# A feed-forward tail: the first pair of the up projection reordered, and the hand-over to the down projection rearranged

## The reference

```python
h = rmsnorm_2(x, norm_ffn_w[l])
u = causal_dwconv(h @ w_up[l], conv_ffn_w[l]) + conv_ffn_b[l]
gate, up = jnp.split(u, 2, axis=-1)
x = x + (jax.nn.silu(gate) * up) @ w_down[l]
return rmsnorm_2(x, norm_final_w)
```

## Time and profile before

| what | value |
|---|---|
| median of 3 runs | 3269.74 us (3268.81 to 3270.42) |
| the profiled execution | 3269.96 us, span 3268.1 us |
| TensorE busy | 3071.9 us, 94% of the span |
| VectorE, ScalarE, GpSimd busy | 1487.5, 815.4, 778.1 us |
| mean granted clock of TensorE | 0.973 |

### The profile page before, as it was taken

How to read it: one execution, slowest core, us unless ns; L and a number is a source line. 1 busy time by engine, 2 the same in 40 slices (tenths; PEclk the granted TensorE clock), 3 DMA queues, 4 the chain that set the end, 5 groups by cost and what they waited for, 6 DMA issues and landing times. The chain is left out here.

```text
span 3268.1 us, 37094 instructions
## 1 busy us (share of the span) xinstructions
PE 3071.9 (94%) x14650; PEld 1742.6 (53%) x14650; DVE 1487.5 (46%) x2481; ACT 815.4 (25%) x1656; POOL 778.1 (24%) x625
## 2 busy tenths in 40 slices
PE   7999999999949999799999998999997999998999
PEld 4457656665424444344456656444444666664444
DVE  2216537674351111524322465314757777774224
ACT  3126524442221111412212126211011222221001
POOL 0004400000000110023022215312606655551323
PEclk8999999999969999899999999999998999999999
DMA  7210000003266987511000130012200112117444
GB/s 291 78 52 29 2 25 2 1 1 136 112 257 244 346 329 270 179 39 39 29 24 28 53 135 2 33 39 82 111 39 39 78 78 78 71 46 284 150 132 135
DMA packets 72316, 334.57 MB, mean 102 GB/s; under 512 B 10960, under 2 KB 12497, under 8 KB 58321
## 3 DMA queue, kind: packets, MB, share of 16 engines
q1 hardware_dynamic: 67536, 315.42, 25.5%
q0 software_dynamic: 4608, 16.78, 2.0%
HBM read 283.92 MB, written 48.23 MB: 102 GB/s over the span
## 5 line engine op out<-in xcount | busy, mean ns | idle before, releaser
L3188 PE MATMUL banks<-down_ring,down_sums 128*128 128x512 f32 x440 | 189.2, 592 | 0.0
L822 PE MATMUL banks<-kT_b,qT_b 96*128 96x512 f32 (+1 forms) x384 | 158.7, 523 | 3.5 <-ACT prob_b L884 2.4
L330 PE MATMUL banks<-w_in,hT 128*128 128x512 f32 (+1 forms) x384 | 157.5, 567 | 1.2 <-PEq L157 1.2
L2905 PE MATMUL banks<-hT,ffn_raw 128*128 128x512 f32 x352 | 156.3, 597 | 1.3 <-PEq L2426 1.3
L728 POOL TENSOR_TENSOR prob<-prob,softmax_columns 128x640 f32<-128x640 f32 (+1 forms) x64 | 75.4, 1199 | 314.6 <-DVE softmax_columns L686 314.6
L3021 DVE SCALAR_TENSOR_TENSOR ffn_acc<-ffn_u,s_ffn_taps,ffn_acc 128x1023 f32<-128x1023 f32 x88 | 129.2, 1479 | 30.4 <-ACT ffn_acc L2962 28.8
L1281 POOL DMA_INDIRECT expert_x<-xn_rows,idxT x16 | 15.7, 983 | 529.6 <-POOLq L1018 522.7
L3188 PEld LDWEIGHTS banks<-down_ring,down_sums 128*128 128x128 f32 x440 | 83.6, 190 | 105.2 <-issue 103.8
L1662 PE MATMUL banks<-hT,side_ring 128*128 128x512 f32 x256 | 127.5, 618 | 1.3 <-PEq L2214 1.3
L1317 PE MATMUL banks<-expert_wg,expert_xT 128*128 128x512 f32 x256 | 114.8, 602 | 2.4 <-ACT expert_xT L1354 1.7
L330 PEld LDWEIGHTS banks<-w_in,hT 128*128 128x128 f32 x384 | 71.8, 190 | 81.8 <-issue 78.5
(11 more groups left out here) (576 smaller groups left out, 6109.8 us busy)
## 6 DMA issues: line engine op xcount, KB each, us to landing
down_ring<-in_w_down SPq DMA_DIRECT2D x132, 256.0 KB, 2.9
expert_wg<-in_w_gate SPq DMA_DIRECT2D x16, 2048.0 KB, 15.2
expert_wu<-in_w_up SPq DMA_DIRECT2D x16, 2048.0 KB, 20.7
expert_wd<-in_w_down SPq DMA_DIRECT2D x16, 2048.0 KB, 8.5
ffn_raw<-in_w_ffn SPq DMA_DIRECT2D x22, 1024.0 KB, 6.1
wmod_slab<-in_w_mod SPq DMA_DIRECT2D x6, 2048.0 KB, 8.0
act_rows<-ffn_acc SPq DMA_DIRECT2D x22, 512.0 KB, 2.6
act_rows<-act_rows SPq DMA_DIRECT2D x22, 512.0 KB, 7.7
```

Of the source, the lines that this page charges most:

```text
L330: last = nc.tensor.matmul(c.ps[:, base + a:base + b], h[:, q, :], k.w_in[i][:, q, 0:b - a], start=q == 0, stop=q == KD - 1)
L822: last = nc.tensor.matmul(scores(u)[:, a:b], heads[u // 2].q[u % 2], heads[u // 2].keys[u % 2][:, a:b], start=True, stop=True, skip_group_ ...
L2905: last = nc.tensor.matmul(c.bank(fi), wt[:, q, :], x[:, q, :], start=q == 0 and m != 2, stop=q == 3, skip_group_check=True)
L3188: return nc.tensor.matmul(c.bank(4 * (p % 2) + t), stationary_of(s)[:, P * t:P * t + P], w[s % RING][:, 0, :], start=j == 0, stop=j == N - 1)
```

## The change

In pair 0 alone TensorE's order becomes 1, 2, 6, 5, 7, 3, 4, and GpSimd's sums come in the order of use: block sums 0, 1 and 2, then four half-width sums for product 6, the in-place one for 7, and four half-width sums each for 7, 3 and 4 (24 instead of 16 instructions, hence the new counts). VectorE makes three of product 6's row sums ahead of T4, and `split(0, 6)` waits for five row sums before its first part and for seven before its last. ScalarE's copies for 6 follow those of product 2.

At the end of `ffn_up` SyncE issues weights for down steps 4 to 7 ahead of rows 10 to 19, GpSimd sums those of steps 4 and 5 as well (`SUMMED` = 6), and the store and read-back of the last two rows leave the stage. In `ffn_down` SyncE first stores these rows from `acc`, issues weights 8 to 11, waits for the store, loads rows 20 and 21, the x tiles and the norm row, and goes on with weights 12.

```diff
     nc = c.nc
-    NP, H, Q, ENDING = NF2 // 2, BANK, BANK // 2, 4
+    NP, H, Q, ENDING, SUMMED, RING = NF2 // 2, BANK, BANK // 2, 4, 6, 8
     w_in = k.ffn_in
     made, rows_summed, w_summed, first_out, corner_out, chained, combined, tapped, conv, silu, done, stored = (
         c.sem(f"ffn_{s}") for s in ("product", "rows_summed", "w_summed", "first_out", "corner_out", "chained", "combined", "tapped", "convolved",
                                     "silu", "done", "stored"))
-    down_summed = c.sem("ffn_down_summed")
+    down_summed = k.down_summed = c.sem("ffn_down_summed")
     B11, B12, B21, B22 = (hT[:, 4 * a:4 * a + 4, H * b:H * b + H] for a in range(2) for b in range(2))
     T1, T2, T4 = (T[:, i, :, :] for i in range(3))
     flat = lambda x: x.rearrange("p q n -> p (q n)")
 
     MADE, COMBINED, SPLIT = 23, 29, (6, 7, 3, 4)
+    ORDER, FIRST_ORDER = (1, 6, 2, 7, 5, 3, 4), (1, 2, 6, 5, 7, 3, 4)
     MADE_AT = {1: 1, 6: 2, 2: 7, 7: 8, 5: 13, 3: 14, 4: 19}
+    FIRST_MADE_AT = {1: 1, 2: 2, 6: 3, 5: 8, 7: 9, 3: 14, 4: 19}
+    FIRST_W, W_AT, FIRST_W_AT = 24, {5: 2, 6: 12, 3: 12, 7: 16, 4: 16}, {5: 2, 6: 10, 7: 16, 3: 20, 4: 24}
     ADDED_AT = {6: 0, 7: 6, 5: 13, 3: 17, 4: 23}
     READ_AT = {6: 4, 7: 10, 3: 21, 4: 27}
     ROWS_AT = {5: 1, 6: 7, 7: 12, 3: 16, 4: 20}
     BANKS = {6: 2, 3: 2, 7: 5, 4: 5}
 
     def ready(p, m, event=0):
-        return MADE * p + MADE_AT[m] + event
+        return MADE * p + (MADE_AT if p else FIRST_MADE_AT)[m] + event
+
+    def w_ready(p, m):
+        return FIRST_W + 16 * (p - 1) + W_AT[m] if p else FIRST_W_AT[m]
 
     def added(p, m, n):
         return COMBINED * p + ADDED_AT[m] + n
             for t in range(2, ENDING):
                 down_weights(t)
             sp.wait_ge(made, MADE * NP)
+            for t in range(ENDING, RING):
+                down_weights(t)
             load(10, 2 * NP - 2)
-            store(NP - 1)
-            sp.wait_ge(stored, 32 * NP)
-            load(2 * NP - 2, 2 * NP)
 
         @block.gpsimd
         def _(pool):
+            def plain_sum(p, i, wait=None):
+                for fi in range(2):
+                    if wait is not None:
+                        pool.wait_ge(w_summed, wait + fi + 1)
+                    out, x, y, op = {0: (sum_of(p, 0, fi), block_of(p, 1, 0, fi), block_of(p, 1, 1, fi), ALU.add),
+                                     1: (sum_of(p, 1, fi), sum_of(p, 0, fi), block_of(p, 0, 0, fi), ALU.subtract),
+                                     2: (sum_of(p, 2, fi), block_of(p, 0, 1, fi), sum_of(p, 1, fi), ALU.subtract),
+                                     7: (block_of(p, 1, 0, fi), block_of(p, 0, 0, fi), block_of(p, 1, 0, fi), ALU.subtract)}[i]
+                    nc.gpsimd.tensor_tensor(out, x, y, op).then_inc(w_summed, 1)
+
+            def sums_of_split(p, ms, at):
+                g = ms[0] in (7, 4)
+                half = slice(0, 2) if len(ms) == 2 else slice(ms[0] in (3, 4), 1 + (ms[0] in (3, 4)))
+                if g:
+                    wide = [raw[p % 2][fi][:, KD:2 * KD, :].rearrange("p (m r) n -> p m (r n)", m=2)[:, half, :] for fi in range(2)]
+                else:
+                    wide = [L1[p % 2][:, 1:3, fi, :, :].rearrange("p m r n -> p m (r n)")[:, half, :] for fi in range(2)]
+                A11, A12, A21, A22 = (wide[fi][:, :, Q * kq:Q * kq + Q] for fi in range(2) for kq in range(2))
+                S1, S2, S4 = (L2[p % 2][g][:, i, half, :, :].rearrange("p m r n -> p m (r n)") for i in range(3))
+                pool.wait_ge(w_summed, at)
+                nc.gpsimd.tensor_tensor(S1, A21, A22, ALU.add).then_inc(w_summed, 1)
+                pool.wait_ge(w_summed, at + 1)
+                nc.gpsimd.tensor_tensor(S2, S1, A11, ALU.subtract).then_inc(w_summed, 1)
+                nc.gpsimd.tensor_tensor(A21, A11, A21, ALU.subtract).then_inc(w_summed, 1)
+                pool.wait_ge(w_summed, at + 2)
+                nc.gpsimd.tensor_tensor(S4, A12, S2, ALU.subtract).then_inc(w_summed, 1)
+
             for p in range(NP):
-                n = 16 * p
                 for fi in range(2):
                     pool.wait_ge(w_in[2 * (p % 2) + fi], 16 * (p // 2 + 1))
                 if p >= 2:
                     pool.wait_ge(made, MADE * (p - 1))
...
-            for t in range(ENDING):
+                n = FIRST_W + 16 * (p - 1) if p else 0
...
+            for t in range(SUMMED):
                 pool.wait_ge(k.down_in[t], 32)
                 nc.gpsimd.tensor_tensor(down[t][:, 0, :], down[t][:, 0, :], down[t][:, 1, :], ALU.subtract).then_inc(down_summed, 1)
...
@@ -2896,7 +2915,7 @@
                     pe.wait_ge(first_out, 2 * p + 2)
                 if m == 5:
                     pe.wait_ge(corner_out, 2 * p + 2)
-                    pe.wait_ge(w_summed, 16 * p + 2)
+                    pe.wait_ge(w_summed, w_ready(p, 5))
...
             def split(p, m):
-                if m in (6, 7):
-                    if p:
-                        pe.wait_ge(combined, added(p - 1, {6: 3, 7: 4}[m], 6))
-                    pe.wait_ge(w_summed, 16 * p + {6: 12, 7: 16}[m])
-                else:
+                if m in (3, 4):
                     pe.wait_ge(combined, added(p, *{3: (6, 6), 4: (7, 7)}[m]))
+                elif p:
+                    pe.wait_ge(combined, added(p - 1, {6: 3, 7: 4}[m], 6))
+                pe.wait_ge(w_summed, w_ready(p, m))
                 if p == 0:
-                    pe.wait_ge(rows_summed, ROWS_AT[m])
+                    pe.wait_ge(rows_summed, ROWS_AT[m] - 2 if m == 6 else ROWS_AT[m])
                 for n in (1, 2, 5, 6, 3, 4, 7):
+                    if p == 0 and m == 6 and n == 7:
+                        pe.wait_ge(rows_summed, ROWS_AT[6])
                     if n in (6, 7):
                         pe.wait_ge(chained, 8 * p + 2 * SPLIT.index(m) + (1 if n == 6 else 2))
                     wt, x = split_factors(p, m, n)
@@ -2925,13 +2945,8 @@
                         last.then_inc(made, 1)
 
             for p in range(NP):
-                plain(p, 1)
-                split(p, 6)
-                plain(p, 2)
-                split(p, 7)
-                plain(p, 5)
-                split(p, 3)
-                split(p, 4)
+                for m in ORDER if p else FIRST_ORDER:
+                    (split if m in SPLIT else plain)(p, m)
...
-                copies(p, 6, 0)
-                copies(p, 6, 1)
+                if p:
+                    copies(p, 6, 0)
+                    copies(p, 6, 1)
                 act.wait_ge(made, ready(p, 2))
                 if p:
                     act.wait_ge(conv, 8 * p)
                 for fi in range(2):
                     nc.scalar.activation(u[:, 0, fi, 0:H], c.bank(fi), ACT.Identity).then_inc(corner_out, 1)
+                if p == 0:
+                    copies(p, 6, 0)
+                    copies(p, 6, 1)
...
+            X11, X12, X21, X22 = halves(T2)
             nc.vector.tensor_tensor(T1, B12, B11, ALU.subtract).then_inc(rows_summed, 1)
             dve.wait_ge(rows_summed, 1)
             nc.vector.tensor_tensor(T2, B22, T1, ALU.subtract).then_inc(rows_summed, 1)
             dve.wait_ge(rows_summed, 2)
+            nc.vector.tensor_tensor(split_rows(6, 0), X12, X11, ALU.subtract).then_inc(rows_summed, 1)
+            dve.wait_ge(rows_summed, 3)
+            nc.vector.tensor_tensor(split_rows(6, 1), X22, split_rows(6, 0), ALU.subtract).then_inc(rows_summed, 1)
+            dve.wait_ge(rows_summed, 4)
+            nc.vector.tensor_tensor(split_rows(6, 2), X21, split_rows(6, 1), ALU.subtract).then_inc(rows_summed, 1)
             nc.vector.tensor_tensor(T4, B21, T2, ALU.subtract).then_inc(rows_summed, 1)
-            split_sums_of(6)
+            dve.wait_ge(rows_summed, 6)
+            nc.vector.tensor_tensor(X12, X22, X12, ALU.subtract).then_inc(rows_summed, 1)
             nc.vector.tensor_tensor(B12, B22, B12, ALU.subtract).then_inc(rows_summed, 1)
             dve.wait_ge(rows_summed, 8)
             split_sums_of(7)
...
+def ffn_down(c, k, d, act_rows, last_rows, w, sums, x, stat, junk, out):
...
-    RING, N, H, READY, ENDING = 8, NF2 // 2, BANK, 4, 4
+    RING, N, H, READY, SUMMED, ENDING = 8, NF2 // 2, BANK, 4, 6, 4
...
-        n_a, n_b = n_a + len(left) - 1, n_b + (len(right) - 1 if s >= READY else 0)
+        n_a, n_b = n_a + len(left) - 1, n_b + (len(right) - 1 if s >= SUMMED else 0)
...
-            for s in range(STEPS):
-                if s >= RING:
-                    wait_used(sp, s - RING)
-                for i, (kh, dh) in enumerate(PRODUCTS[s // N][2] if s >= READY else ()):
+            for f in range(2 * N - 2, 2 * N):
+                sp.dma_start(k.act_dram[f], last_rows[f % 2]).then_inc(rows_out, 16)
+            for s in range(RING, STEPS):
+                wait_used(sp, s - RING)
+                for i, (kh, dh) in enumerate(PRODUCTS[s // N][2]):
```

(21 more changed lines are left out.)

33 lines of the change are left out of this document (13 added, 20 removed).

## The result

The changed kernel takes 3252.18 us (median of 6 executions, 3249.37 to 3259.69), the kernel before 3269.56 in the same session. The ratio is 0.995, 95% interval 0.9937 to 0.9963: 16.3 us less, 12.1 to 20.6. The forecast was 21.5 us less. The direction was right and the gain is some 5 us smaller: from the median of 3269.74 the ratio gives 3253.4, just above the range's upper end of 3253.

What follows compares the result with a forecast made beforehand. TensorE, busy 94% of the span, bounds the kernel, so only its idle stretches pay: 12.1 us at the first pair plus 9.4 at the hand-over make 21.5, from 3269.74 to 3248.2 us, range 3241 to 3253.

Steps and rivals of the forecast that it cites:

- Pair 0's sums: First pair: GpSimd's and VectorE's sums take 21.4 us, so product 6 is let go at 2487.7 (bounds 2485 and 2489.9).
- the model of turns: First pair: GpSimd and VectorE alternate; GpSimd's turn costs 1.27 or 0.73 us, VectorE's 2.06 or 0.43.
- The hand-over: Up to down stage: TensorE idle 1.1 us at full clock instead of 12.38; gain 9.4 us including the step 12 stall.
- a wait of SyncE for the stores that costs nothing: Down stage: stores seen landed at about 3004.5, while weights 8 to 11 keep the queue full until 3009.
- Rival 5: Down stage: SyncE's wait for stores holds up x tiles and weights 12 onwards; landed at 3034 gives 3277.7; chance 0.02.
- Is another wait next?: First pair behind product 6: products 5, 7 and 3 and pair 1's product 6 were all expected without a wait.
- pairs 1 to 10 carry the shift through unchanged: Up projection: full pairs of 44.82 us just move earlier, so the two stretches' gains add.
- 4.6 us of cover: Pair 0: VectorE's adds of 6 end at 2504.2, ahead of product 3 at 2508.8.
- GpSimd, with 12 sums ..., is done by 2521: Pair 1: 12 sums of at most 1.5 us from 2503 finish before product 6 is due at 2527.7; no wait.
- the slow start of product 6: Pair 0: first 8 records after the idle stretch take 3.78 us instead of 1.89; kept as before.
- the stall at step 12: Down stage: TensorE waits 3.5 us for weights 12, then loses 1.6 us to the slow clock.

Runs made afterwards that it cites:

- experiment 4: Changed kernel with product 5 ahead of product 6 in pair 0: 3251.01 us, ratio 0.9944 to the kernel before.
- experiment 7: Changed kernel with ScalarE's first copy for product 4 of pair 0 ahead of its tap: 3255.55 us, ratio 0.9958 to the kernel before.
- experiment 9: Changed kernel with weights 12 and 13 early, GpSimd's last four pair 1 sums held for VectorE's taps, ScalarE's product 4 copy before its tap: 3244.59 us.
- experiment 10: Changed kernel with weights 12 and 13 early, GpSimd held for VectorE's taps, ScalarE's copy before its tap, product 5 ahead of 6: 3242.38 us.
- Experiment 6: Changed kernel with weights 12 and 13 early and GpSimd's last four pair 1 sums held until VectorE's four pair 0 taps are done: 3244.38 us.
- experiment 5: Changed kernel run again, unedited: 3252.24 us, ratio 0.9955 to the kernel before.
- experiment 2: Hand-over part of the change alone, pair 0 as in the kernel before: 3259.73 us, ratio 0.9971 to the kernel before.
- experiment 1: First pair's part of the change alone, hand-over as in the kernel before: 3261.76 us, ratio 0.9978 to the kernel before.
- experiment 8: Changed kernel with weights 12 and 13 early and GpSimd's pair 1 sums held until VectorE's first four product 7 adds: 3250.22 us.

## Why the prediction was right and wrong

**Right.** Pair 0's sums: the model of turns put product 6 at 2487.7, and it started at 2487.32. The hand-over: 1.20 us idle at full clock (forecast 1.1), step 12 the next to wait, for weights that stand behind two stores, the read-backs and the x tiles (landing 44.9 us after pair 10, forecast 45.3), and a wait of SyncE for the stores that costs nothing. Rival 5, which needed those stores late, had nothing in the trace for it.

**Wrong: "Is another wait next?" in the first pair, and the step from it that pairs 1 to 10 carry the shift through unchanged.** The forecast followed VectorE only as far as the adds of product 6, which free the banks of product 3. It found 4.6 us of cover there, and the trace agrees: these adds end at 2503.2 and product 3 starts at 2509.38, without a wait. But the queue goes on: adds of 7, of 5, of 3, then ScalarE's tap, ScalarE's copy for product 4 behind it, VectorE's four taps, and only then the adds that pair 1 needs. With TensorE 10 us ahead, this chain is the bound from product 4 of pair 0 into pair 1. Its head is TensorE's product 7: VectorE waits 2.98 us for it and then has next to none (0.19 us) up to 2517.8, so TensorE can gain about that much before VectorE's own work is the bound. The forecast put the waits behind product 3 at nothing; they were 1.23 us in product 4 and 2.00 in pair 1, which makes pair 1 2.3 us longer. Experiments 4, 7, 9 and 10 show it: each removes a wait of TensorE ahead of the chain's end, and another comes behind it.

**Stopped too early: "GpSimd, with 12 sums ..., is done by 2521".** The 12 sums that product 6 of pair 1 needs were done at 2518.6, in time as forecast. But four more follow them, and VectorE's taps had moved 10 us forward, to beside these four: the taps took 8.59 us instead of 5.11, and GpSimd ended at 2526.6. Experiment 6 shows that this is the whole of pair 1's 2.0 us as long as product 4 waits ahead of it; where that wait is taken out too (experiment 9), 1.46 us come back in pair 1. The forecast had looked at GpSimd's due time and not at what it would stand beside.

**Mis-sized: the slow start of product 6.** It was kept at 8.14 us and took 9.15. The clock fell as before and stayed down longer: before, it was 0.50 from 2493 to 2496 and 0.74 from 2496 to 2498. The windows of the changed kernel:

```profile
2487.30:2490.00 2.70, 2.68 (x6) 2.18 (x7) 2.70 (x3) 0.38 (x1) 2.70 (x2) 0.50 0.00 0
2490.00:2493.00 3.00, 3.00 (x8) 2.36 (x7) 2.97 (x3) 0.00 (x0) 2.84 (x4) 0.50 0.00 0
2493.00:2495.00 2.00, 2.00 (x10) 1.71 (x9) 2.00 (x3) 0.38 (x1) 2.00 (x2) 0.89 0.00 0
```

**Mis-sized: the stall at step 12.** 2.80 us and no slow clock in the profiled execution, where 3.5 and 1.6 were counted, hence 11.4 for 9.4. In other executions the slow clock cost 1.8 (experiment 5), 3.1 (experiment 2), 3.0 (experiment 4, behind 3.85 us) or nothing (experiment 7), so 1.6 is a fair middle, and the part alone measured 9.5. That the clock held in the profiled execution is luck of that execution and hides some of the shortfall in pairs 0 and 1.

The shortfall, from the profiled executions: 1.0 (slow start), 1.2 (product 4), 2.3 (pair 1), 1.0 (pair 10), less 2.0 at the hand-over, makes 3.5; the spans' shortfall is 21.5 - 18.3 = 3.2, since some 0.4 us was won outside these stretches. Pair 10's wait was 1.31 in one execution of the changed kernel and 0.29 in the other; it was 1.35 in experiment 4 and 0.3 or less in all other traces, 0.26 in the kernel before. So it goes with the execution and not with the change; what makes it is open.

**Left open.** By the medians the gain is smaller still than by the profiled executions. The changed kernel's runs reach 3259.69, 8.1 above the profiled one. Part of that spread is not the change's: the kernel before spread over 1.6 us in the first six runs, but over 6.1, 3.9 and 5.4 us on the chips of the experiments. A long add (5.70 and 5.09 us) moved the start of pair 2 by 4.3 us in experiment 1 and 3.8 in experiment 8, about half of the 8.1. In experiment 1 the execution that had it was 4.3 us above the median; in experiment 8 it was the shortest of five. It fell in no profiled execution of the changed kernel, so that it makes the long runs is argued and not shown. What decides whether an add stands for four turns was not found.

## What to carry to other kernels

When a stall of the bounding engine is shortened, follow each helper's queue to its last entry before the next wait, not only to the first thing that is due: here the adds of product 6 had cover and the entries behind them did not. A moved instruction is also a moved neighbour: ask what it will now run beside on the other engines, and hold the one that is not urgent (one wait on GpSimd gave back 2.0 us). And where a queue holds urgent weights behind a wait and bulk loads that nobody needs yet, look for the place where the urgent ones can go first: moving two weights ahead took away a stall of 2.8 us. Before filling an idle stretch of the bounding engine, look for the idle time of the helper that follows: it tells how much of the stretch can be won (here 2.98 us of VectorE's, and 2.5 at the first tap, out of 5.9).
